# Four reduction pieces of each feed-forward output kept to the end and done token tile by token tile, in a four-block float32 transformer kernel

## The chip, the cores and the metric

One core of a Trainium2 chip runs the whole program in one launch. The metric is the device time of one execution in microseconds (us), the median over several executions. TensorE is written PE in the profile (its weight loads PEld), VectorE is DVE, ScalarE is ACT, GpSimd is POOL and SyncE is SP.

## What is computed

The input x has 256 tokens of 1024 features. It goes through two blocks of a first kind and then two of a second kind, everything in float32. Cut to what matters here:

```python
# first kind, twice
x = layer_norm(ALPHA * x + mix, ln1_g[i], ln1_b[i])              # mix: attention and spatial gating
gate, up = jnp.split(x @ w_ffn_in[i], 2, axis=-1)                # D_FF = 2816
ffn = (jax.nn.silu(gate) * up) @ w_ffn_out[i]
ple = (p[i] @ w_ple[i]) * jax.nn.sigmoid(x @ w_ple_gate[i])
x = layer_norm(ALPHA * x + ffn + ple, ln2_g[i], ln2_b[i])
# second kind, twice
mod = silu(c) @ ada_w[layer] + ada_b[layer]                      # sh1, sc1, g1, sh2, sc2, g2
h = rms_norm(x, norm_mix[layer]) * (1 + sc1) + sh1
x = x + g1 * mixer(h)
h = rms_norm(x, norm_mlp[layer]) * (1 + sc2) + sh2
a = jax.nn.relu(h @ mlp_w1[layer])                               # 4096 wide
x = x + g2 * ((a * a) @ mlp_w2[layer])
```

## The kernel before, in words

**Tokens and matmuls.** The 256 tokens are two token tiles t = 0 and 1 of 128. A product of float32 precision is made of three matmuls: an operand is divided into a high part (the rounded value) and a low part (the rest), and high x high, high x low and low x high are added in PSUM (lines 1375 to 1377). The activations transposed for this lie in XTH/XTL (the stage's input, 8 pieces of 128 features) and HTH/HTL (the feed-forward's inner values, 8 pieces).

**Weights.** All weights are streamed from HBM once, in the order of `plan()` (line 46). A chunk of the plan is cut into items of at most 2048 elements per partition (1 MB). There are 9 buffers of that size (NBUF, line 20); RAW and WB are two views of the same memory. SP loads an item into one buffer (`load`, line 1262). `split` then uses a second buffer: ACT writes the high part into it (line 1501, recorded as line 1497, WB<-RAW) and DVE replaces the raw value by the low part (line 1699). An item in use therefore holds two buffers, until its last matmul, and an item that is only loaded holds one.

**The planner.** The order of every instruction is written out once by the Python code: `do(part, ...)` appends to one list, and each engine executes its own part of that list in this order. `advance()` (line 312) splits items ahead of their use until `cur["ahead"]` reaches `cur["pairs"]`, which is 3. `loads()` (line 304) puts loads into the list ahead of that; its condition is quoted here, because the change touches what it gives:

```python
while cur["load"] < len(seq) and most and cur["load"] - cur["item"] < NBUF - 2 * cur["pairs"] and bufs:
```

With `pairs` 3 this lets 9 - 6 = 3 loads lie ahead of the item that is split next. A load waits only for what frees its own buffer, but SP issues loads in list order. `used()` (line 338) gives an item's two buffers back with the event of its last matmul.

**The ada items.** The weights of the `mod` product are not for PE. They are items of 1 MB as well, put one by one behind other items (lines 275 to 287), and DVE multiplies them into an accumulator with four instructions (`ada`, lines 1745 to 1760; source lines 1755 and 1758). An ada item has no split; when the planner comes to it, it appends the ada step to the list and its buffer is free again when DVE has done it. There are 8 ada chunks of two items in each first-kind feed-forward and 8 in the first second-kind MLP; the second MLP has none.

**A feed-forward of the first kind** (lines 836 to 896). For c = 0 to 10 the input product of chunk c (two items of w_ffn_in, 24 matmuls each over both tiles) is made; between its two items the inner values of chunk c-1 are transposed (`ffn_turn`, source line 1400 on PE, ACT makes HTH, DVE makes HTL at line 1780). After it `partial()` (line 455) adds chunk c-1 times w_ffn_out (one item, 24 matmuls) into four PSUM banks. Its inner values come out of PSUM by ACT (Silu, GB<-ps) and DVE (line 1994). In all pieces but the last two, `partial` does an item for both tiles. The last two, d = 9 and 10, are done at the end tile by tile: both items for tile 0, `last(0)`, both items for tile 1, `last(1)`. `last` adds the sum to x (line 2002), and takes the layer norm: statistics (1961, 1964), reciprocal root on POOL (1297, 1299), and two passes (1971, 1974). The transposition of tile 0's result for the next stage stands between tile 1's statistics and its passes (`between`, line 880). In the second layer (i = 1) it is not a plain transposition: `norm_tile` (648) squares x on ACT, takes the root on POOL and scales x into MIX on DVE (1979), and `go` (662) transposes MIX and applies scale and shift, half on ACT and half on DVE (1800), before XTH and XTL (1805) are made.

**An MLP of the second kind** (lines 1198 to 1246) is built alike with 8 chunks: two items of mlp_w1 and two of mlp_w2 per chunk, each transposition two halves (1.0 us of PE), Relu and Square on ACT. Only the last piece, d = 7, is done tile by tile; `last` multiplies by the gate and adds (2058, 2062).

**The joint.** The next stage starts in `linear2` (line 411): its first item for tile 0, then `mid()`, which holds the transposition of tile 1, then more of tile 0, then tile 1. `pad` is a number of 128x512 matmuls on constants whose result is not used (`busy`, source line 1360); they stand ahead of a wait.

## Time and profile before

| what | value |
|---|---|
| median of 3 executions | 1452.9 us |
| lowest and highest of these | 1451.3 and 1455.47 us |
| the profiled execution, its own time | 1450.07 us |
| its span, first to last instruction | 1448.3 us |
| mean granted TensorE clock | 0.981 |
| busy, share of the span: PE, PEld, DVE, ACT, POOL | 93, 77, 65, 45 and 8% |
| read from HBM | 267.75 MB, 186 GB/s over the span |

The profile covers one execution. Its times are us from the span's start unless ns is said. "idle before <-releaser" names what an engine waited for. The granted clock is a share of full speed: 1.00 is 2.4 GHz and 0.50 is 1.2 GHz. Matmuls overlap, so the step from one start to the next counts, not the recorded duration.

### The profile page before, as it was taken

What the parts mean: (1) busy time and instruction counts of PE and PEld (TensorE: products, weight loads), DVE (VectorE), ACT (ScalarE), POOL (GpSimd) and SP (SyncE); (2) the same over time, 40 slices, a digit from 0 to 9 for tenths busy, and PEclk for the clock granted to TensorE, in tenths of its full rate; (3) what the DMA queues carried; (4) which work ended last, traced back from release to release, by engine and by line L of the source; (5) the groups of instructions that cost most, each with busy time, mean ns of one, the idle gap of its engine ahead of it and who ended that gap; (6) DMA issues with size and microseconds to landing.
All of it is one profiled execution on the core that took longest, in us unless ns stands there. A gap on an engine that the chain in (4) does not pass through costs nothing.

```text
span 1448.3 us, 16560 instructions
## 1 busy us (share of the span) xinstructions
PE 1352.1 (93%) x6683; PEld 1111.1 (77%) x6715; DVE 943.2 (65%) x1249; ACT 656.9 (45%) x886; POOL 113.7 (8%) x156
## 2 busy tenths in 40 slices
PE   6999999999989999999789898999998978899998
PEld 6767888887967788887589776888876766688886
DVE  4856777766675777774657856766765775554444
ACT  4544533333553543334366444544435544454542
POOL 1010000000020000000223300000003330000000
PEclk9999999999999999999999999999999988999999
DMA  8505677772713567774153204776753430355550
GB/s 345 209 1 203 231 292 290 293 285 98 269 59 116 207 260 291 291 298 181 41 192 135 102 1 145 269 284 248 281 225 141 151 115 1 116 203 178 188 186 29
DMA packets 40236, 269.87 MB, mean 186 GB/s; under 512 B 4544, under 2 KB 4688, under 8 KB 11872
## 3 DMA queue, kind: packets, MB, share of 16 engines
q1 hardware_dynamic: 37712, 259.31, 48.1%
q0 software_dynamic: 2304, 8.46, 1.6%
q8 instruction: 53, 0.87, 0.2%
q10 hardware_dynamic: 144, 1.05, 0.2%
q14 instruction: 23, 0.19, 0.0%
HBM read 267.75 MB, written 1.05 MB: 186 GB/s over the span
## 4 chain that ended last, share of the span: by engine, by line
PE 78%; DVE 11%; ACT 5%; issue 2%; POOL 2%; DMA 1%; DVEq 0%; ACTq 0%; POOLq 0%
PE ps L1375 23%; PE ps L1377 23%; PE ps L1376 23%; PE ps L1400 4%; DVE WB L1699 2%; ACT E L1497 1%; PE ps L1484 1%; PE ps L1388 1%; POOL st L1299 1%; ACT WB L1497 1%; PE ps L1460 1%; DVE st L1893 1%; PE ps L1360 1%; ACT XTH L1497 1%; DVE st L1961 1%
## 5 line engine op out<-in xcount | busy, mean ns | idle before, releaser
L1699 DVE TENSOR_TENSOR WB<-RAW,WB 128x2048 fp32r<-128x2048 f32 (+5 forms) x210 | 453.3, 2161 | 271.7 <-ACT WB L1497 271.5
L1375 PE MATMUL ps<-WB,XTH 128*128 128x512 f32 (+3 forms) x1176 | 457.3, 389 | 33.3 <-DVE XTL L1704 14.0
L1497 ACT ACTIVATE WB<-RAW 128x2048 fp32r<-128x2048 f32 (+5 forms) x210 | 379.8, 1809 | 237.5 <-PE ps L1377 223.1
L1377 PE MATMUL ps<-WB,XTL 128*128 128x512 f32 (+3 forms) x1176 | 447.9, 381 | 0.0
L1376 PE MATMUL ps<-WB,XTH 128*128 128x512 f32 (+3 forms) x1176 | 447.2, 380 | 0.0
L1375 PEld LDWEIGHTS ps<-WB,XTH 128*128 128x128 f32 x1176 | 222.7, 189 | 75.7 <-DVE XTL L1704 14.0
L1377 PEld LDWEIGHTS ps<-WB,XTL 128*128 128x128 f32 x1176 | 222.5, 189 | 38.7
L1376 PEld LDWEIGHTS ps<-WB,XTH 128*128 128x128 f32 x1176 | 223.0, 190 | 34.8
L1375 PE MATMUL ps<-WB,HTH 128*128 128x512 f32 (+1 forms) x452 | 179.3, 397 | 3.2 <-DVE HTL L1780 3.2
L1376 PE MATMUL ps<-WB,HTH 128*128 128x512 f32 (+1 forms) x452 | 178.5, 395 | 0.0
L1377 PE MATMUL ps<-WB,HTL 128*128 128x512 f32 (+1 forms) x452 | 178.5, 395 | 0.0
L1758 DVE SCALAR_TENSOR_TENSOR ACC<-RAW,colv,ACC 128x512 f32<-128x512 f32 x168 | 126.2, 751 | 5.1
L1497 ACT ACTIVATE HTH<-ps 128x512 fp32r<-128x512 f32 (+1 forms) x58 | 32.1, 585 | 163.3 <-PE ps L1400 163.1
L1297 POOL TENSOR_SCALAR st<-st 128x1 f32<-128x1 f32 (+3 forms) x42 | 25.6, 610 | 1016.1 <-DVE st L1964 540.4
L1375 PEld LDWEIGHTS ps<-WB,HTH 128*128 128x128 f32 x452 | 85.9, 190 | 22.7 <-DVE HTL L1780 3.7
L1377 PEld LDWEIGHTS ps<-WB,HTL 128*128 128x128 f32 x452 | 85.8, 190 | 19.6
L1376 PEld LDWEIGHTS ps<-WB,HTH 128*128 128x128 f32 x452 | 86.0, 190 | 19.1
L1497 ACT ACTIVATE GB<-ps 128x512 f32<-128x512 f32 (+1 forms) x94 | 46.5, 500 | 91.6 <-PE ps L1377 91.5
L1497 ACT ACTIVATE E<-ps,st 128x128 f32<-128x128 f32 (+1 forms) x104 | 42.5, 421 | 80.1 <-DVE st L1903 80.1
L1360 PE MATMUL ps<-cstb 128*128 128x512 bf16 x227 | 64.4, 401 | 1.9 <-issue 0.2
L1780 DVE TENSOR_TENSOR HTL<-ps,HTH 128x512 fp32r<-128x512 f32 x54 | 35.8, 688 | 39.9 <-ACT HTH L1497 39.9
L1299 POOL TENSOR_TENSOR st<-st,cst 128x1 f32<-128x1 f32 (+3 forms) x42 | 48.1, 1145 | 3.5
(173 smaller groups left out, 1055.2 us busy)
## 6 DMA issues: line engine op xcount, KB each, us to landing
RAW<-W SPq DMA_DIRECT2D x220, 1024.0 KB, 4.9
RAW<-W SPq DMA_DIRECT2D x7, 960.0 KB, 4.7
RAW<-W SPq DMA_DIRECT2D x6, 910.0 KB, 6.5
RAW<-W SPq DMA_DIRECT2D x9, 576.0 KB, 3.5
VEC<-vecd POOLq DMA_DIRECT2D x10, 512.0 KB, 6.0
RAW<-W SPq DMA_DIRECT2D x8, 512.0 KB, 3.3
RAW<-W SPq DMA_DIRECT2D x6, 546.0 KB, 7.0
GB<-xTd ACTq DMA_DIRECT2D x1, 1024.0 KB, 8.4
```

The costliest lines, as they stand in the source:

```text
L1297: eng.tensor_scalar(x, x, scale, eps, ALU.mult, ALU.add).then_inc(*own.up())
L1299: eng.tensor_tensor(x, x, MH.to_broadcast([128, x.shape[1]]), ALU.pow).then_inc(*up("rsqrt", key))
L1360: eng.matmul(banks[b][:, :], identb, cstb[:, 0:512], start=True, stop=True)
L1375: eng.matmul(ps, xh, hi[:, j, c0:c0 + cw], start=first and j == 0, stop=False)
L1376: eng.matmul(ps, xh, lo[:, j, c0:c0 + cw], start=False, stop=False)
L1377: op = eng.matmul(ps, xl, hi[:, j, c0:c0 + cw], start=False, stop=last and j == n - 1)
L1388: op = eng.matmul(banks[b][:, q:q + 1], ACC[:, a, q * 128:q * 128 + 128], ones[:, 0:1], start=True, stop=True)
L1400: op = eng.transpose(banks[b][0:rows, j * 128:j * 128 + 128], src, ident)
L1497: return eng.activation(dst, src, f, **k)
L1699: eng.tensor_tensor(WB[:, it["raw"], 0:w], RAW[:, it["raw"], 0:w], WB[:, it["high"], 0:w].bitcast(F32), ALU.subtract).then_inc(*up("wl", n))
L1758: op = eng.scalar_tensor_tensor(out=ACC[:, a, :], in0=view[:, j, :], scalar=cond[:, kt:kt + 1], in1=ACC[:, a, :], op0=ALU.mult, op1=ALU.add)
L1780: eng.tensor_tensor(HTL[:, r2:r2 + 2, :], banks[b][:, :].rearrange("p (n q) -> p n q", n=2), HTH[:, r2:r2 + 2, :].bitcast(F32), ALU.subtra ...
```

## The change

The plan keeps the w_ffn_out pieces 7 to 10 to the end (before, 9 and 10 alone were done tile by tile, and every piece had its place in the plan behind the input product of the next chunk), and the mlp_w2 pieces 6 and 7 (before: 7). The last `partial` has then four items per tile in all three kinds of stage. From c = 8 (first kind) and c = 6 (second kind) `cur["pairs"]` is 4, until the last `partial` is over. `partial` takes a table `before` of steps that are put in front of item n of tile t: the last transposition in front of (0, 1) or (0, 2), splits of the next stage in front of (1, 1), the second half of the normalisation in front of (1, 2), and tile 0's transposition for the next stage in front of (1, 3). The pads of 14, 10, 11 and 6 matmuls at the joints become 3, 3, 3 and 2; the pad of 11 ahead of each MLP stays.

```diff
@@ plan()
-            if c:
-                out.append(("w_ffn_out", i, (c * 256 - 256, c * 256), [(0, 1024)]))
+            for d in [c - 1] if 0 < c <= 7 else range(7, 11) if c == 11 else []:
+                out.append(("w_ffn_out", i, (d * 256, d * 256 + 256), [(0, 1024)]))
...
-            if c:
-                out.append(("mlp_w2_2", i, (c * 512 - 512, c * 512), [(0, 1024)]))
+            for d in [c - 1] if 0 < c <= 6 else range(6, 8) if c == 8 else []:
+                out.append(("mlp_w2_2", i, (d * 512, d * 512 + 512), [(0, 1024)]))
@@ partial()
-        def partial(name, parts, ps, first, last, evac=None):
+        def partial(name, parts, ps, first, last, evac=None, before={}):
...
                     for n in range(len(its)):
+                        if (t, n) in before:
+                            before[t, n]()
                         one(n, t)
@@ norm_tile()
-        def norm_tile(t, after):
+        def norm_start(t, after):
             g = uid()
             ss = col(1)
             do("norm_sq", g, t, ss, after)
             do("rsqrt", ("nt", g), ss, 1.0 / D, 1e-6, ("norm_sq", g))
+            return g, t, ss
+
+        def norm_end(g, t, ss):
             do("norm_apply", g, t, ss)
             hn[t] = ("hn", g)
+
+        def norm_tile(t, after):
+            norm_end(*norm_start(t, after))
@@ start of the second layer
-                run(linear2("w_in", "x", xt_w, puts[0:2], mid_in, pad=(6, 0)))
+                run(linear2("w_in", "x", xt_w, puts[0:2], mid_in, pad=(2, 0)))
@@ feed-forward of the first kind
+            for c in range(11):
+                if c == 8:
+                    cur["pairs"] = 4
...
+                gen = linear("w_ffn_in", "x", xt_w, put)
+                next(gen)
                 if c:
-                    d = c - 1
...
-                if c < 11:
-                    run(gen)
+                    part_ = ffn_turn(c - 1)
+                run(gen)
                 if c:
...
-                    if d < 9:
-                        ht_free[d % 2] = [partial("w_ffn_out", [part_], acc4, d == 0, False)]
-                    elif d == 9:
-                        part9 = part_
+                    if c - 1 < 7:
+                        ht_free[(c - 1) % 2] = [partial("w_ffn_out", [part_], acc4, c == 1, False)]
+                    else:
+                        kept.append(part_)
...
+            kept.append((4, []))
...
+            def turn_last():
+                kept[-1][1].extend(ffn_turn(10)[1])
+                gb_free[:] = f_free[0] + [("ffn", (i, 10, 0)), ("ffn", (i, 10, 1))]
+                if i:
+                    do("lambdas", col(2), list(scr["free"]))
+                    scr["free"] = [("lam_dot", 0)]
+                    then["mod"] = norm_mod(0, 0, list(gb_free))
+
+            def tile0():
+                if i:
+                    then["mod"][1](0, pad=3)
+                else:
+                    xt_w[0][:] = to_XT(X, 8, x_n[0], 0)
 
             def last(t, done):
...
-                def between():
-                    if t and i == 0:
-                        xt_w[0][:] = to_XT(X, 8, x_n[0], 0)
-                    elif t:
-                        norm_tile(0, x_n[0])
-                        go(0, pad=14)
-
-                x_n[t] = ln_tile((i, 2, t), t, [("add_out", (i, t, c)) for c in range(2)], between)
-                if t:
-                    advance(1)
-                if t and i == 1:
-                    norm_tile(1, x_n[1])
-
-            t_pe = [partial("w_ffn_out", [part9, part_], acc4, False, True, last)]
+                x_n[t] = ln_tile((i, 2, t), t, [("add_out", (i, t, c)) for c in range(2)])
+                if i:
+                    then["norm"] = norm_start(t, x_n[t])
+                    if t:
+                        norm_end(*then["norm"])
...
+            t_pe = [partial("w_ffn_out", kept, acc4, False, True, last,
+                            {(0, 1): turn_last, (1, 1): lambda: advance(1),
+                             (1, 2): (lambda: norm_end(*then["norm"])) if i else lambda: advance(1), (1, 3): tile0})]
+            cur["pairs"] = 3
@@ starts of the two second-kind layers
-                            pad=(10, 0)))
+                            pad=(3, 0)))
...
-                                                                  for c in range(2)], mid, pad=(11, 0)), part((2, 3))),
+                                                                  for c in range(2)], mid, pad=(3, 0)), part((2, 3))),
@@ MLP of the second kind
+            gen = linear2("mlp_w1_2", "x", xt_w, [put_f(0), put_f(1)], mid, pad=(11, 0))
+            next(gen)
+            for c in range(1, 8):
+                if c == 6:
+                    cur["pairs"] = 4
...
+                part_ = mlp_turn(c - 1)
+                run(gen)
...
+                if c - 1 < 6:
+                    ht_free[(c - 1) % 2] = [partial("mlp_w2_2", [part_], acc4, c == 1, False)]
...
+            kept = [part_, (4, [])]
+
+            def turn_last():
+                kept[1][1].extend(mlp_turn(7)[1])
+                if i == 0:
+                    then["mod"] = norm_mod(1, 0, f_free[1] + [("sq", (0, 7, 0)), ("sq", (0, 7, 1))])
 
             def last(t, done):
-                if t and i == 0:
-                    go(0)
                 for c in range(2):
                     gated_put(i, c, 1, xg)(t, acc4[t][c][0], done[c])
-                if t:
-                    advance(1)
-                if i == 0:
-                    norm_tile(t, xg[t])
+                if i:
+                    do("store", t, xg[t])
                 else:
-                    do("store", t, xg[t])
-
-            t_pe = [partial("mlp_w2_2", [part_], acc4, False, True, last)]
+                    then["norm"] = norm_start(t, xg[t])
+                    if t:
+                        norm_end(*then["norm"])
+
+            before = {(0, 2): turn_last}
+            if i == 0:
+                before.update({(1, 1): lambda: advance(1), (1, 2): lambda: norm_end(*then["norm"]),
+                               (1, 3): lambda: then["mod"][1](0, pad=3)})
+            t_pe = [partial("mlp_w2_2", kept, acc4, False, True, last, before)]
+            cur["pairs"] = 3
```

`mlp_turn` is the old transposition of a chunk as a function, and `ffn_turn` in the first kind likewise.

## Rows read from the trace of the kernel before

**Rows 1.** The page: busy time of each engine, share of the span, instructions.
```profile
PE 1352.1 (93%) x6683; PEld 1111.1 (77%) x6715; DVE 943.2 (65%) x1249; ACT 656.9 (45%) x886; POOL 113.7 (8%) x156
```

**Rows 2.** Timeline of PE, joint after the first feed-forward (start, us, idle before).
```profile
339.63 0.63 PE L1400 MATMUL ps<-cst,GB 128*128 128x128 f32 x4 [1.02 <-DVE GB L1994]
...
351.06 0.40 PE L1377 MATMUL ps<-WB,HTL 128*128 128x512 f32 x1
...
358.45 1.04 PE L1400 MATMUL ps<-cst,X 128*128 128x128 f32 x8
```

**Rows 3.** Timeline of PE, joint after the second feed-forward.
```profile
694.07 0.40 PE L1377 MATMUL ps<-WB,HTL 128*128 128x512 f32 x1
...
701.25 1.09 PE L1400 MATMUL ps<-cst,MIX 128*128 128x128 f32 x8 [3.75 <-DVE MIX L1979]
...
707.61 0.41 PE L1375 MATMUL ps<-WB,XTH 128*128 128x384 f32 x1 [1.42 <-DVE XTL L1805]
...
713.01 1.09 PE L1400 MATMUL ps<-cst,MIX 128*128 128x128 f32 x8 [2.08 <-DVE MIX L1979]
```

**Rows 4.** Timeline of PE, first MLP: its last transposition's product and the joint.
```profile
1078.65 0.47 PE L1375 MATMUL ps<-WB,HTH 128*128 128x512 f32 x1 [1.62 <-DVE HTL L1780]
...
1089.89 1.04 PE L1400 MATMUL ps<-cst,MIX 128*128 128x128 f32 x8
...
1102.51 1.97 PE L1400 MATMUL ps<-cst,MIX 128*128 128x128 f32 x8 [2.92 <-DVE MIX L1979]
```

**Rows 5.** Chain that ended last: small products at chunk ends, first feed-forward and first MLP.
```profile
291.50 0.79 PE ps L1388 x8
...
309.37 0.79 PE ps L1388 x8
...
1027.54 0.79 PE ps L1388 x8
...
1051.41 0.79 PE ps L1388 x8
```

**Rows 6.** Timeline of DVE at the start of chunk 8, first feed-forward.
```profile
293.55 2.29 DVE L1699 TENSOR_TENSOR WB<-RAW,WB 128x2048 fp32r<-128x2048 f32 x1 [1.06 <-ACT WB L1497]
295.76 0.48 DVE L1755 TENSOR_SCALAR ACC<-RAW,colv 128x512 f32<-128x512 f32 x1
296.28 2.33 DVE L1758 SCALAR_TENSOR_TENSOR ACC<-RAW,colv,ACC 128x512 f32<-128x512 f32 x3
298.96 0.69 DVE L1780 TENSOR_TENSOR HTL<-ps,HTH 128x512 fp32r<-128x512 f32 x1 [0.36 <-ACT HTH L1497]
...
302.98 3.11 DVE L1758 SCALAR_TENSOR_TENSOR ACC<-RAW,colv,ACC 128x512 f32<-128x512 f32 x4
```

**Rows 7.** SP's waits, 290 to 310 us; landing of two loads then; of the last load.
```profile
SPq L1266 <- DVE ACC L1758: 13.4, 2, 6.7
...
DMA to landing us min/median/max: 4.8/5.9/6.9
...
DMA to landing us min/median/max: 4.8/4.8/4.8
```

**Rows 8.** Groups by line and shape: count, then busy us, mean ns of one.
```profile
L1497 ACT ACTIVATE WB<-RAW 128x2048 fp32r<-128x2048 f32 x172 | 329.0, 1913 | 192.9 <-PE ps L1377 188.2 <-DMA RAW<-W 4.6
...
L1497 ACT ACTIVATE GB<-ps 128x256 f32<-128x256 f32 x44 | 17.0, 385 | 57.6 <-PE ps L1377 57.6
L1994 DVE TENSOR_TENSOR GB<-GB,ps 128x256 f32<-128x256 f32 x44 | 16.9, 415 | 5.8 <-ACT GB L1497 5.8
...
L1497 ACT ACTIVATE GB<-GB 128x512 f32<-128x512 f32 x32 | 20.2, 632 | 1.0
L1497 ACT ACTIVATE MIX<-X 128x1024 f32<-128x1024 f32 x8 | 8.5, 1059 | 28.6 <-DVE X L2062 17.8 <-DVE X L1974 10.8
```

**Rows 9.** Granted clock by stretch of 1 us, the column before the last two.
```profile
1102.00:1103.00 1.00, 0.49 (x3) 0.49 (x4) 1.00 (x2) 0.00 (x0) 1.00 (x2) 0.50 0.00 0
...
1105.00:1106.00 1.00, 1.00 (x5) 0.77 (x5) 0.13 (x1) 0.81 (x2) 1.00 (x4) 0.83 0.00 0
```

More of the change, by code:

```diff
@@ L835, in program, with ffn_turn, put @@
             acc4 = None
-            for c in range(12):
-                if c < 11:
-                    def put(t, b, done, c=c):
-                        do("ffn", (i, c, t), t, c, b, done, f_free[c % 2])
-                        give(b, ("ffn", (i, c, t)))
-                    gen = linear("w_ffn_in", "x", xt_w, put)
-                    next(gen)
-                if c:
-                    d = c - 1
-                    r2 = 2 * (d % 4)
-                    b, fr = take()
-                    g = uid()
-                    do("ffn_turn", g, [GB[:, t, (d % 2) * 256 + kt * 128:(d % 2) * 256 + kt * 128 + 128]
-                                       for kt in range(2) for t in range(2)], r2, b,
-                       [("ffn", (i, d, t)) for t in range(2)] + fr, ht_free[d % 2])
-                    give(b, ("tl", g))
-                    f_free[d % 2] = [("tp", g)]
-                if c < 11:
-                    run(gen)
+            kept = []
+            def ffn_turn(d):
+                r2 = 2 * (d % 4)
+                b, fr = take()
+                g = uid()
+                do("ffn_turn", g, [GB[:, t, (d % 2) * 256 + kt * 128:(d % 2) * 256 + kt * 128 + 128]
+                                   for kt in range(2) for t in range(2)], r2, b,
+                   [("ffn", (i, d, t)) for t in range(2)] + fr, ht_free[d % 2])
+                give(b, ("tl", g))
+                f_free[d % 2] = [("tp", g)]
+                return r2, [("tl", g)]
+            for c in range(11):
+                if c == 8:
+                    cur["pairs"] = 4
+                def put(t, b, done, c=c):
+                    do("ffn", (i, c, t), t, c, b, done, f_free[c % 2])
+                    give(b, ("ffn", (i, c, t)))
+                gen = linear("w_ffn_in", "x", xt_w, put)
+                next(gen)
+                if c:
+                    part_ = ffn_turn(c - 1)
+                run(gen)
                 if c:
@@ L1196, in put_f, with mlp_turn @@
                 return put
-            for c in range(9):
-                if c == 0:
-                    gen = linear2("mlp_w1_2", "x", xt_w, [put_f(0), put_f(1)], mid, pad=(11, 0))
-                    next(gen)
-                    continue
-                if 2 <= c < 8:
+            def mlp_turn(d):
+                los = []
+                for hf in range(2):
+                    b, fr = take()
+                    g = uid()
+                    r2 = 4 * (d % 2) + 2 * hf
+                    do("ffn_turn", g, [GB[:, t, (d % 2) * 512 + (hf * 2 + kt) * 128:(d % 2) * 512 + (hf * 2 + kt) * 128 + 128]
+                                       for kt in range(2) for t in range(2)], r2, b,
+                       [("sq", (i, d, t)) for t in range(2)] + fr, ht_free[d % 2])
+                    give(b, ("tl", g))
+                    los.append(("tl", g))
+                f_free[d % 2] = [("tp", g)]
+                return 4 * (d % 2), los
@@ L1204, in program @@
+            gen = linear2("mlp_w1_2", "x", xt_w, [put_f(0), put_f(1)], mid, pad=(11, 0))
[3 more added lines that the diff above has]
+                    cur["pairs"] = 4
+                if c > 1:
                     gen = linear("mlp_w1_2", "x", xt_w, put_f(c))
                     next(gen)
[L1206 to L1218 removed]
@@ new lines, in program @@
+                run(gen)
+                if acc4 is None:
+                    acc4 = [[take(), take()], [take(), take()]]
+                if c - 1 < 6:
+                    ht_free[(c - 1) % 2] = [partial("mlp_w2_2", [part_], acc4, c == 1, False)]
+            xg = [[], []]
+            then = {}
+            kept = [part_, (4, [])]
[3 more added lines that the diff above has]
+                    then["mod"] = norm_mod(1, 0, f_free[1] + [("sq", (0, 7, 0)), ("sq", (0, 7, 1))])
@@ L1244, in program @@
+            before = {(0, 2): turn_last}
[4 more added lines that the diff above has]
+            cur["pairs"] = 3
+            if i == 0:
+                mod, go = then["mod"]
             x_w = xg
```

40 lines of the change are left out of this document (7 added, 33 removed).

## The prediction

> **What bounds the kernel now.** I read the page first: PE is busy for 93% of 1448.3 us [rows 1], so a gain can only come from the gaps of PE. The timeline of PE shows where they are. Inside the weight-streaming stages there are none: a chunk takes 17.9 us from one small product to the next, which is three items of 5.6 us and the transposition and small product, 1.1 us, and in the first MLP 23.9 us, four items of 5.5 us and 1.8 us [rows 5]. The gaps that the change is about lie at the joints. After the first feed-forward, 1.0 us ahead of the last transposition, and 7.15 us from the last product's end (351.3) to tile 1's transposition (358.45) [rows 2]. After the second, 18.7 us from 694.3 to 713.01, only part of it work [rows 3]. After the first MLP, 12.6 us from 1089.89 to 1102.51 [rows 4]. The end of the program has no joint behind it.
>
> Then I read what feeds PE. SP waits for DVE's ada work, two waits of 6.7 us in 20 us [rows 7], and DVE shows a split (2.3), an ada step (2.9), HTL, a split and the next ada step (3.1) [rows 6]. With three loads ahead nobody notices that wait. That is the row to look at, because the change takes the loads ahead from three to one.
>
> **Part 1, `pairs` 4.** In the quoted condition 9 - 2x4 is 1. A load enters the list only when everything loaded has been split or, for an ada item, done. Two pairs of buffers freed by one item now both become high parts. I follow the list from chunk 8 of the first feed-forward, where M = 291.5 us is the end of piece 6 [rows 5]. In8a and in8b are split, in9a, ada A and in9b are loaded. The list becomes: split in9a, ada A, split in9b, load ada B, ada B, load in10a. Load ada B uses ada A's buffer, load in10a uses ada B's. DVE ends ada A at 298.65, as before [rows 6]. Then in series: ada B lands 4.8 later, the time of a lone 1 MB load [rows 7], at 303.5; DVE has it done 3.1 later at 306.6 [rows 6]; in10a lands 4.8 later at 311.4; its ACT half ends at 313.3 [rows 8]. In ACT's list the split of in10a stands ahead of the Silu of chunk 8, and on DVE its low half stands ahead of line 1994. So: ACT 313.3, DVE low half 315.6, two products 316.5 [rows 6, 8]. PE wants them for the transposition of chunk 8, behind in9a, at 292.3 + 3x5.6 + 0.35 = 309.4. It stands idle for 7.1 us. Behind it, in10a and in10b are split in time and no later load has an ada item in front: no further stall in this stage.
>
> After such a gap the clock is low. Once PE had stood for nearly 3 us, the clock was 0.50 (1.2 GHz) from 1102 and was back by about 1105.3 [rows 4, 9]: 3.3 us at half speed, 1.6 us lost. The sum takes 1.6 for each long gap that ends a chain; its bounds are 0 (no drop) and 3.3 (twice as long). Both feed-forwards have ada items at chunk 8, so 2 x (7.1 + 1.6) = **17.4 us**.
>
> The sum by a lone load's 4.8 us is for the last load of the program. The Trainium skill (DMA: Bandwidth & Descriptors, Anatomy of one DMA) fits another issuing path with about 2.0 us plus bytes at 436 GB/s, which would be 4.4 us; by it the seven serial loads counted here and below would cost 2.8 us less in all.
>
> **Part 2, the first MLP.** M = 1027.5 is the end of the second item of piece 4 [rows 5]. The same list: ada A done M + 7.1, ada B landed 11.9, done 15.1, in7a landed 20.0. HTL of chunk 5 stands behind ada B: 16.4, PE wants it at 0.8 + 5.5 + 1.0 + 5.5 = 12.8, with the real gaps 12.6: 3.8 us. Then ada items stand between pieces 6a and 6b and behind it. The load of the first waits for piece 5a (M + 22.3) and DVE is through at 33.9; 6b lands 38.8, ACT 40.7, DVE 43.0, second ada 46.1, HTL of chunk 6 47.4. PE wants it at 40.4: 7.0 us. Piece 7a is loaded into that ada's buffer and lands at 51.0, ACT 52.9; four Relu and Square of 0.63 [rows 8] 55.4; PE wants the last transposition at 53.0: 2.4 us. HTL 7 comes behind the split of 7b, at 61.0, against 56.5: 4.5 us, of which 1.6 is there now [rows 4], because this transposition stands in front of (0, 2) and is needed at once. Sum 3.8 + 7.0 + 2.4 + 2.9 = 16.1, and one drop of the clock, 1.6; earlier drops fall into the next wait: **17.7 us**. These are list orders times row durations; the links are bounded by 0 (all hidden) and by landing times of 6.9 instead of 4.8 us, which the second of two loads close together has [rows 7], some 2 us for each of seven loads.
>
> **Part 3, the joints.** Moving products does not change their number; tile 1 has now four items, 11.2 us, beside tile 0's chain. But the joint ends with tile 1's chain, which is as long as before.
> *First joint.* The last transposition no longer waits: gain 1.2 with its issue. Tile 1's chain loses the 1.2 us of XTL halves from its middle and starts some 0.3 late: 6.2 instead of 7.15 [rows 2]. Tile 0's transposition, 1.05 us, now stands in the products. Net gain 1.2 - 1.05 + 0.95 = 1.1, say 1.2 with the shorter pad.
> *Second.* The split put in front of (1, 1) stands on ACT behind tile 0's square (1.06) [rows 8] and on DVE ahead of tile 0's scaling: norm 6.25 (as long as tile 1's 6.2 above), square 7.45, ACT split 9.25, DVE 11.45, scaling 12.2 us after tile 0's last product. PE reaches tile 0's transposition at 8.4 + pad 0.7 = 9.1: a new stall of 3.1. From the new end of the products tile 1's transposition follows 11.9 us later instead of 18.7 [rows 3]; that end is 1.05 + 0.7 + 3.1 later, and 1.2 are saved at the last transposition: 18.7 - 11.9 - 4.85 + 1.2 = 3.1. Three splits, not two, are then ahead of tile 1's scale and shift: -1.1. Gain 2.0.
> *Third.* Tile 1's transposition follows 8.3 instead of 12.6 us [rows 4] after the products; the end is 1.75 later: 2.5. Behind it PE waits 1.2 for a split and 2.5 for XTL, where it now loses 0.6: together a loss of 0.6.
> *Fourth, the program's end:* no ada items in that MLP; a load is issued at an item's end, lands 4.8 us later and is wanted after 5.5. The wait of 1.6 stays. 0.
> Joints: **-2.6 us**, bounded by 0 and by -12 (if no split were in the way). Pads: fewer constants, 0 on the path, since each stands in a wait.
>
> **Sum.** 17.4 + 17.7 - 2.6 = 32.5. On the profiled execution's 1450.07 that is 1482.6; it lies 2.8 below the median, and the forecast is 1452.9 + 32.5, about **1485 us**.
>
> **Rivals.**
> *A: the first MLP hides its chain,* since its chunk is 6 us longer than the feed-forward's for the same two ada items [rows 5]. Against: HTL stands behind ada B in DVE's list whatever the chunk's length. 1452.9 + 17.4 - 2.6 = 1468. 0.09.
> *B: faster.* The place is DVE's ada B at chunk 8: if its load were already under way, PE sees no gap, and only the joints change; with tile 0's normalisation covered by 11.2 us and splits out of its way they give up to 12: 1441; with my own joints 1450. It decides at 7 us: the chain from ada A's end to the GB product is 17.8 us long and must shrink to 10.7. For it: today SP's waits cost nothing. Against: the condition allows one load. 0.11 in all, 0.07 of it beyond 0.3%.
> *C: the clock falls more.* The pads of 14 and 11 at the joints are gone and each joint keeps a wait of 3 to 6 us; already with pads it fell once [rows 9]. Five more half-speed stretches at 1.6 and some loads at 6.9: 1485 + 8 + 6 = 1499. 0.12. By the Trainium skill (TensorE: Matmul & The Clock Gate, What's actually happening) the throttled clock is the default and activity releases it; that rule speaks for this rival.
>
> **How the numbers follow.** Forecast 0.68, A 0.09, B 0.11, C 0.12. A measurement tells 0.3%, 4.4 us, from no change. Faster 0.07, same 0.04, slower 0.89. The forecast's own bounds are 1485 - 1.6x3 - 9 (joints) = 1471 and 1485 + 15 = 1500; with A in, 1466 to 1500. B and the far ends of C are left out.
>
> **What would show it.** In the profile after: a wait of PE at line 1400 for DVE GB of 6 to 8 us at chunk 8 of both feed-forwards, ACT waiting for DMA just ahead of it, DVE's ada step waiting for DMA; HTL waits of 4, 7 and 4.5 us in the first MLP; no 1.0 us wait at the feed-forwards' last transposition, the 1.6 one left in both MLPs; granted clock below 0.981. The prediction is wrong if PE has no wait at chunk 8 of the feed-forwards, or if ACT never waits there for DMA.

## The result, and the profile after

The changed kernel takes **1484.7 us** (median of 4 runs, 1483.4 to 1488.8), the kernel before 1452.1 (4 runs, 1450.9 to 1455.5): a ratio of 1.0225, with a 95% interval of 1.0207 to 1.0242. It is 32.6 us slower. The chips differ by up to 2 us, so each experiment has its own runs of the kernel before. The profiled execution of the changed kernel took 1485.46 us and has a span of 1483.7.

The page of the changed kernel, first the line that answers to [rows 1], then the share of the chain that ended last, then three groups of section 5:

```profile
PE 1365.6 (92%) x6688; PEld 1122.1 (76%) x6688; DVE 942.3 (64%) x1249; ACT 655.4 (44%) x886; POOL 118.2 (8%) x156
...
PE 72%; DVE 14%; ACT 6%; DMA 4%; issue 3%; POOL 2%; SPq 0%; ACTq 0%; DVEq 0%; POOLq 0%
...
L1407 PE MATMUL ps<-WB,XTH 128*128 128x512 f32 (+3 forms) x1176 | 462.2, 393 | 31.4 <-DVE XTL L1736 14.2
...
L1407 PE MATMUL ps<-WB,HTH 128*128 128x512 f32 (+1 forms) x452 | 182.7, 404 | 13.5 <-DVE HTL L1812 13.5
...
L1790 DVE SCALAR_TENSOR_TENSOR ACC<-RAW,colv,ACC 128x512 f32<-128x512 f32 x168 | 126.2, 751 | 13.9 <-DMA RAW<-W 8.8
```

DVE and ACT do the same work in the same time. PE has the same products, but 27 fillers fewer at the joints: 41 before, 14 now, since the third joint has also got 3 ahead of tile 0's transposition, where it had none. (The counts of the page, 6688 and 6683, do not show this, as some records of products are missing from a trace.) A filler takes 0.21 us from one start to the next, by the first of these two groups of PE's timeline at the third joint. It is of the kernel before, the second of the changed one:

```profile
1090.98 2.32 PE L1360 MATMUL ps<-cstb 128*128 128x512 bf16 x10
...
1124.87 0.81 PE L1392 MATMUL ps<-cstb 128*128 128x512 bf16 x3
```

So PE had 5.8 us less to do, and it is busy for 13.5 us longer all the same (1365.6 against 1352.1 in [rows 1]): its products run slower. PE's busy time inside the stretches with a granted clock of 0.50, halved, is what they lost: 22.4 us before and 41.3 after, 18.9 more. The span grew by 35.4 us, of which 21.9 are time in which PE is idle. DMA has 4% of the chain, which had 1% of it before.

The waits of ACT for loads, over the whole execution (total us, times, longest), and then those of PE for the two tiles that the forecast named. Lines are shifted by the change: 1407 to 1409 are the products, 1432 the transpositions, 1812 HTL, 2026 the GB product, 1731 and 1529 the two halves of a split, 1787 and 1790 the ada step.

```profile
ACT WB L1529 <- DMA RAW<-W: 83.6, 18, 12.7
```

```profile
PE ps L1407 <- DVE HTL L1812: 15.0, 6, 4.3
...
PE ps L1432 <- DVE GB L2026: 12.3, 2, 6.2
```

Before, ACT waited for loads 7 times, 14.2 us in all, the longest 6.6; PE 3.2 us for HTL and 2.0 for GB. The chain of waits can be read at chunk 8 of the first feed-forward. The timeline of DVE, which answers to [rows 6]:

```profile
296.37 2.29 DVE L1731 TENSOR_TENSOR WB<-RAW,WB 128x2048 fp32r<-128x2048 f32 x1 [1.05 <-ACT WB L1529]
298.58 0.48 DVE L1787 TENSOR_SCALAR ACC<-RAW,colv 128x512 f32<-128x512 f32 x1
299.09 2.33 DVE L1790 SCALAR_TENSOR_TENSOR ACC<-RAW,colv,ACC 128x512 f32<-128x512 f32 x3
...
306.33 3.11 DVE L1790 SCALAR_TENSOR_TENSOR ACC<-RAW,colv,ACC 128x512 f32<-128x512 f32 x4 [2.71 <-DMA RAW<-W]
309.37 0.68 DVE L1812 TENSOR_TENSOR HTL<-ps,HTH 128x512 fp32r<-128x512 f32 x1
316.22 2.29 DVE L1731 TENSOR_TENSOR WB<-RAW,WB 128x2048 fp32r<-128x2048 f32 x1 [6.17 <-ACT WB L1529]
318.43 0.74 DVE L2026 TENSOR_TENSOR GB<-GB,ps 128x256 f32<-128x256 f32 x2
```

The timeline of ACT there, and that of PE:

```profile
314.28 1.91 ACT L1529 ACTIVATE WB<-RAW 128x2048 fp32r<-128x2048 f32 x1 [12.53 <-DMA RAW<-W]
316.10 0.64 ACT L1529 ACTIVATE GB<-ps 128x256 f32<-128x256 f32 x2
```

```profile
310.10 0.50 PE L1407 MATMUL ps<-WB,XTH 128*128 128x512 f32 x1 [0.77 <-DVE HTL L1812]
...
319.32 1.08 PE L1432 MATMUL ps<-cst,GB 128*128 128x128 f32 x4 [6.17 <-DVE GB L2026]
```

Ada A ends at 301.4. Ada B starts when its load lands, at 306.33, 4.9 us later, and ends at 309.4; the load of in10a, which uses its buffer, lands at 314.28, again 4.8 later. Only then do ACT, DVE and at last PE go on. From the small product (PE has its last product before it until 294.33) to the end of the GB products there are 24.9 us.

To see where the time went, take one instruction of PE that both kernels have and compare its start. This table is worked out from the timelines of PE; "added" is the step of the difference from the row above.

| instruction of PE | before | after | difference | added |
|---|---|---|---|---|
| first small product of the first feed-forward | 184.12 | 186.94 | 2.8 | 2.8 |
| transposition of H after the first joint | 388.01 | 399.13 | 11.1 | 8.3 |
| first small product of the second feed-forward | 527.15 | 538.75 | 11.6 | 0.5 |
| transposition of MIX after the second joint | 731.90 | 749.94 | 18.0 | 6.4 |
| first small product of the first MLP | 914.24 | 930.67 | 16.4 | -1.6 |
| transposition of modc after the third joint | 1123.87 | 1156.52 | 32.6 | 16.2 |
| end | 1448.3 | 1483.7 | 35.4 | 2.8 |

The three changed places that bring time are worth 8.3 + 6.4 + 16.2 = 30.9 us. The other 4.5 arise in the rows between, where both kernels do the same but for the second MLP, in the last one. What the slow clock took from PE's busy time grew by 14.4 us in the three rows and by 4.5 in the others, so the granted clock, which fell at other moments (below), accounts for them. The medians, which average over that, differ by 32.6.

The three waits of the first MLP, in the timeline of PE (the second and the third answer to [rows 4]), with the transposition between them:

```profile
1061.03 0.77 PE L1407 MATMUL ps<-WB,HTH 128*128 128x512 f32 x1 [4.34 <-DVE HTL L1812]
...
1091.27 0.76 PE L1407 MATMUL ps<-WB,HTH 128*128 128x512 f32 x1 [3.71 <-DVE HTL L1812]
...
1099.55 1.03 PE L1432 MATMUL ps<-cst,GB 128*128 128x128 f32 x8
...
1104.40 0.77 PE L1407 MATMUL ps<-WB,HTH 128*128 128x512 f32 x1 [3.81 <-DVE HTL L1812]
```

The joints, which answer to [rows 2] (tile 1's transposition) and [rows 3] (tile 0's and tile 1's), again in PE's timeline:

```profile
362.32 0.40 PE L1409 MATMUL ps<-WB,HTL 128*128 128x512 f32 x1
...
368.77 1.06 PE L1432 MATMUL ps<-cst,X 128*128 128x128 f32 x8 [3.07 <-DVE X L2006]
...
714.10 1.43 PE L1432 MATMUL ps<-cst,MIX 128*128 128x128 f32 x8 [2.64 <-DVE MIX L2011]
...
719.18 0.39 PE L1409 MATMUL ps<-WB,HTL 128*128 128x512 f32 x1
...
729.71 1.97 PE L1432 MATMUL ps<-cst,MIX 128*128 128x128 f32 x8 [5.95 <-DVE MIX L2011]
```

From the last product's end to tile 1's transposition there are 6.05 us at the first joint (7.0 before) and 10.1 at the second (18.5 before). The joints did get shorter; and tile 0's transposition at the second waits for 2.64 us.

The granted clock (the column before the last two), in stretches of 1 us, at chunk 8 and after the wait of the first joint:

```profile
321.00:322.00 1.00, 1.00 (x4) 0.74 (x3) 0.98 (x2) 1.00 (x2) 0.00 (x0) 0.50 0.01 0
...
324.00:325.00 1.00, 1.00 (x6) 0.82 (x5) 1.00 (x1) 0.38 (x1) 0.00 (x0) 1.00 0.00 0
369.00:370.00 1.00, 1.00 (x10) 1.00 (x9) 1.00 (x1) 0.57 (x2) 0.00 (x0) 0.99 0.00 0
370.00:371.00 1.00, 1.00 (x5) 1.00 (x5) 1.00 (x2) 0.52 (x2) 0.00 (x0) 0.50 0.00 0
...
373.00:374.00 1.00, 1.00 (x6) 1.00 (x6) 0.00 (x0) 0.00 (x0) 0.57 (x1) 0.80 0.00 0
```

At 0.50 (1.2 GHz) PE does 4 or 5 instructions in 1 us, at 1.00 (2.4 GHz) 6 to 10. Summed over all stretches of 1 us from 10 us on, what is missing to 1.00 comes to 27.9 us before and 51.4 after; part of it lies in waits, where it costs nothing, and the 41.3 and 22.4 us above are the part in which PE was at work.

### The profile page after: what moved, and what is told of

Read it like the earlier page. It is cut to its first block, busy times and chain, and to the rows that moved or that the text cites. A ratio compares the mean times of both kernels' runs of the same rounds, so it can differ in the third digit from the quotient of the medians.

```text
span 1483.7 us, 16531 instructions
## 1 busy us (share of the span) xinstructions
PE 1365.6 (92%) x6688; PEld 1122.1 (76%) x6688; DVE 942.3 (64%) x1249; ACT 655.4 (44%) x886; POOL 118.2 (8%) x156
## 4 chain that ended last, share of the span: by engine, by line
PE 72%; DVE 14%; ACT 6%; DMA 4%; issue 3%; POOL 2%; SPq 0%; ACTq 0%; DVEq 0%; POOLq 0%
PE ps L1407 21%; PE ps L1409 21%; PE ps L1408 21%; PE ps L1432 4%; DMA RAW<-W 4%; DVE WB L1731 3%; ACT WB L1529 2%; DVE ACC L1790 2%; ACT E L1529 1%; PE ps L1516 1%; PE ps L1420 1%; PE ps L1492 1%; PE ps L1392 1%; POOL st L1331 1%; DVE st L1925 1%
## 5 line engine op out<-in xcount | busy, mean ns | idle before, releaser
L1407 PE MATMUL ps<-WB,XTH 128*128 128x512 f32 (+3 forms) x1176 | 462.2, 393 | 31.4 <-DVE XTL L1736 14.2
L1407 PEld LDWEIGHTS ps<-WB,XTH 128*128 128x128 f32 x1176 | 225.8, 192 | 74.5 <-DVE XTL L1736 14.6
L1408 PEld LDWEIGHTS ps<-WB,XTH 128*128 128x128 f32 x1176 | 225.8, 192 | 35.3
L1407 PE MATMUL ps<-WB,HTH 128*128 128x512 f32 (+1 forms) x452 | 182.7, 404 | 13.5 <-DVE HTL L1812 13.5
L1408 PE MATMUL ps<-WB,HTH 128*128 128x512 f32 (+1 forms) x452 | 180.8, 400 | 0.0
L1407 PEld LDWEIGHTS ps<-WB,HTH 128*128 128x128 f32 x452 | 87.7, 194 | 34.1 <-DVE HTL L1812 14.7
L1408 PEld LDWEIGHTS ps<-WB,HTH 128*128 128x128 f32 x452 | 87.6, 194 | 19.6
```

Of the source, the lines that this page charges most:

```text
L1407: eng.matmul(ps, xh, hi[:, j, c0:c0 + cw], start=first and j == 0, stop=False)
L1408: eng.matmul(ps, xh, lo[:, j, c0:c0 + cw], start=False, stop=False)
```

## The experiments

All ratios are to the kernel before on the same chip.

### Which term is which: the switch to four pairs, later

**e1.** Both switches are moved, 8 to 10 in the feed-forwards and 6 to 7 in the MLPs.

```
-                if c == 8:
+                if c == 10:
                     cur["pairs"] = 4
...
-                if c == 6:
+                if c == 7:
                     cur["pairs"] = 4
```

> The changed kernel with one edit: the four pairs start at chunk 10 instead of 8 in both feed-forwards, and at chunk 7 instead of 6 in both MLPs. Everything else of the change stays. Theory S (the stalls come from loads that go one by one past the ada items): in the feed-forwards the GB wait of 6.2 us, the HTL wait of 0.8 and the slow products behind them (1.4) vanish, 2 x 8.3 = 16.6 us; in the first MLP the wait for the HTL of chunk 5 (4.3) and its slow products (2.5) vanish, and of the two later ones (3.7 and 3.8, with 4 us of slow products) at least half goes, since the loads of the first ada item and of piece 6b are under way before the switch: 7 + 5 = 12. 1484.7 - 16.6 - 12 = 1456, within 1450 to 1462. Rival K (the kept pieces and the splits packed ahead of the joints cost the time, whenever the switch comes): no less than 1475.

**e2.** Only the first of the two edits.

> The same edit in the two feed-forwards alone (chunk 10 instead of 8); the MLPs keep the switch at chunk 6. It parts the two terms of the prediction. Theory S: 1484.7 - 16.6 = 1468, and the three HTL waits of the first MLP stay at 4.3, 3.7 and 3.8 us. If the MLP's share were small (rival A of the prediction), e1 and this one would agree within 3 us.

Measured: e1 1458.2 us (10 runs, ratio 1.0030, 1.0018 to 1.0043), e2 1465.9 us (4 runs, ratio 1.0084, 1.0058 to 1.0111). So the late switch in the feed-forwards alone gives back 18.8 us of the 32.6 (16.6 expected), and that in the MLP another 7.7 (12 expected). Taken against the kernel before on the same chip, e2 gives back 19.6. The sum for e1 was 1456, and 1458.2 is within its range. In e1's list of PE's waits no wait for DVE's GB is left, and of HTL this:

```profile
PE ps L1407 <- DVE HTL L1812: 9.4, 3, 4.2
```

The wait for the HTL of chunk 5 is gone, as expected. Those of chunks 6 and 7 are still there, in PE's timeline of e1:

```profile
1063.73 0.61 PE L1407 MATMUL ps<-WB,HTH 128*128 128x512 f32 x1 [3.59 <-DVE HTL L1812]
...
1071.65 1.07 PE L1432 MATMUL ps<-cst,GB 128*128 128x128 f32 x8 [0.55 <-ACT GB L1529]
...
1076.93 0.76 PE L1407 MATMUL ps<-WB,HTH 128*128 128x512 f32 x1 [4.22 <-DVE HTL L1812]
```

I had expected half of them to go. The last ada items stand between the kept pieces 6a, 6b and 7a, so the chain of single loads only starts one chunk later; e6 below takes them out of that place. Rival K, that the kept pieces themselves cost the time, wanted 1475 or more, and falls. Rival A of the prediction, that the MLP hides its chain, falls too: e1 and e2 differ by 7.7 us, and e2's waits of PE for HTL still come to 14.5 us, where the kernel before has 3.2.

### Four pairs without the kept pieces

**e3.** The kernel before, with the switch and its way back, at the places where the changed kernel has them.

```
             for c in range(12):
+                if c == 8:
+                    cur["pairs"] = 4
...
             t_pe = [partial("w_ffn_out", [part9, part_], acc4, False, True, last)]
+            cur["pairs"] = 3
...
             for c in range(9):
+                if c == 6:
+                    cur["pairs"] = 4
...
             t_pe = [partial("mlp_w2_2", [part_], acc4, False, True, last)]
+            cur["pairs"] = 3
```

> The kernel before with nothing but four pairs of buffers from chunk 8 of each feed-forward and chunk 6 of each MLP until their last partial is done; no piece is kept back. Theory S says where four pairs alone bite: in the MLP the list of items is the same in both kernels, so the three waits come here too, 12 to 16 us; in the feed-forward piece 7 still stands among the products of chunk 8 and gives the chain from the first ada step to the GB product (24.9 us after the small product) 5.7 us more cover, 22.8 instead of 17.1, so that 0 to 3 us are left for each: 1452 + 14 + 3 = 1469, within 1464 to 1475. Rival P (four pairs cost the same wherever they stand): 1482 or more. Rival K (the kept pieces cost it): 1452 to 1456.

Measured: 1475.3 us (4 runs, ratio 1.0142, 1.0111 to 1.0173), 22.4 us slower than before; expected were 17, and the range ended at 1475, so it is just outside. Compared by the same method as in the table, the MLP costs 13.8 us (12 to 16 expected) and each feed-forward 5.5 (0 to 3 expected). The miss is in the feed-forward. The timeline of DVE in e3 and the wait in that of PE:

```profile
300.17 2.28 DVE L1705 TENSOR_TENSOR WB<-RAW,WB 128x2048 fp32r<-128x2048 f32 x1
305.32 3.11 DVE L1764 SCALAR_TENSOR_TENSOR ACC<-RAW,colv,ACC 128x512 f32<-128x512 f32 x4 [2.86 <-DMA RAW<-W]
308.35 0.68 DVE L1786 TENSOR_TENSOR HTL<-ps,HTH 128x512 fp32r<-128x512 f32 x1
```

```profile
309.08 0.50 PE L1381 MATMUL ps<-WB,HTH 128*128 128x512 f32 x1 [3.64 <-DVE HTL L1786]
```

I had looked for the end of the chain, the GB product, and found it covered by piece 7. It is. But HTL of chunk 7 stands behind ada B in DVE's list, and piece 7 wants it at 305.45: a wait of 3.64 us, and its 24 products then take 7.4 us instead of 5.75. Without the kept pieces the single load costs 22 us; the change as a whole costs 33.

### The ada item or the single load

**e5.** The changed kernel with its switches where they are; only the ada chunks of the feed-forwards are moved one chunk forward in the plan.

```
-            if 1 <= c <= 8:
-                ada(*ADA[i * 8 + c - 1])
+            if c <= 7:
+                ada(*ADA[i * 8 + c])
```

> The changed kernel with the switch to four pairs left at chunk 8 and chunk 6; only the ada items of each feed-forward stand one chunk earlier (with chunks 0 to 7 instead of 1 to 8), so that none is left in the list once a single load goes ahead. Theory S (it is the ada item in the chain of single loads, not the single load by itself): the waits of 6.2 and 0.8 us at chunk 8 vanish in both feed-forwards, with their clock: as the run with the late switch in the feed-forwards, 1466, within 1463 to 1470. Rival L (one load ahead is too few for PE by itself, since a 1 MB load takes 4.8 us, ACT and DVE 4.1 and a piece of products 5.7): the waits move to chunks 9 and 10 and the time stays above 1475.

Measured: 1464.6 us (4 runs, ratio 1.0076, 1.0050 to 1.0102), 1466 expected. No wait for GB is among PE's, and its waits for HTL are the MLPs' alone (13.8 us). It is as good as e2, by an edit that does not touch the number of loads ahead. This settles the mechanism in the feed-forwards: one load ahead is enough for PE as long as every item in the list is split; the ada item, which has to be done before its buffer is free, turns it into a chain load, ada, load, split. Rival L (a single load is too little by itself) falls.

### The fillers

**e4.** The changed kernel with the fillers that stand in `linear2` at the three joints at their length of before. These are 19 of the 27 that the change took away. The 14 ahead of tile 0's transposition at the second joint stay at 3.

```
-                run(linear2("w_in", "x", xt_w, puts[0:2], mid_in, pad=(2, 0)))
+                run(linear2("w_in", "x", xt_w, puts[0:2], mid_in, pad=(6, 0)))
...
-                            pad=(3, 0)))
+                            pad=(10, 0)))
...
-                                                                  for c in range(2)], mid, pad=(3, 0)), part((2, 3))),
+                                                                  for c in range(2)], mid, pad=(11, 0)), part((2, 3))),
```

> The changed kernel with the lengths of the filler products at the three joints put back to those of before (6, 10 and 11 instead of 2, 3 and 3); the switch stays at chunk 8 and 6. Theory S: fillers lie in waits, no change beyond the clock: 1484.7 - 0 to 3. Rival C (the shorter fillers let the clock fall at the joints): the half-speed stretches at 370, 714, 728 and 1134 us go and the time falls by 5 us or more, to 1480 or less.

Measured: 1487.3 us (4 runs, ratio 1.0228, 1.0203 to 1.0253), not faster than the changed kernel (1.0225). In one place the clock did what rival C says: in e4 it stays up behind the wait of the first joint,

```profile
370.00:371.00 1.00, 0.78 (x7) 0.81 (x8) 1.00 (x2) 0.12 (x1) 0.00 (x0) 1.00 0.00 0
...
373.00:374.00 1.00, 1.00 (x8) 1.00 (x7) 1.00 (x3) 0.29 (x1) 0.13 (x1) 1.00 0.00 0
```

That the fillers held it there is not shown. In the profiled executions of e1, e2, e6 and e7 the clock stays at 1.00 behind the same wait (3.08 to 3.12 us) with the short fillers of the changed kernel; in those of e5 and e8, with the same fillers and the same wait (3.08), it falls, and in that of e10, with no filler and a wait of 3.54, it falls for 6.8 us. And ahead of that joint, at chunk 8, where nothing was edited, e4's clock falls for longer (5.1 us missing to 1.00 instead of 3.4). The total does not move: as a remedy, longer fillers in `linear2` do nothing.

### Removing what is left

**e6.** e1, and the 24 ada chunks spread 9, 9 and 6, where they were 8, 8 and 8.

```
-            if 1 <= c <= 8:
-                ada(*ADA[i * 8 + c - 1])
+            if c <= 8:
+                ada(*ADA[i * 9 + c])
...
-            if i == 0 and c < 8:
-                ada(*ADA[16 + c])
+            if i == 0 and c < 6:
+                ada(*ADA[18 + c])
```

> The run with the late switch in all stages (1458.2), and the 24 ada chunks spread 9, 9 and 6 over the chunks 0 to 8 of the feed-forwards and 0 to 5 of the first MLP, where they were 8, 8 and 8: none stands among the last pieces of the MLP. Theory S: the waits of the first MLP for the HTL of chunk 6 (3.6 us), for the Squares of chunk 7 (0.55) and for the HTL of chunk 7 (4.2, of which 1.6 was there before the change) fall to 1.6, with some 3 us of half-speed products: 1458.2 - 6.8 - 3 = 1448.5, within 1446 to 1451. Rival D (the single load, or the 11th chunk's DVE work with ada items in chunk 0, costs as much elsewhere): 1455 or more.

Measured: **1446.1 us** (6 runs, ratio 0.9956, 0.9942 to 0.9970), 12.1 us less than e1, at the lower end of the range of 1446 to 1451. So the mechanism holds in the first MLP too: without ada items among the single loads its waits are gone, and rival D falls. Of PE's waits for HTL the two of 1.6 us are left that the kernel before has:

```profile
PE ps L1407 <- DVE HTL L1812: 3.2, 2, 1.6
```

**e9.** The kernel before with this plan, nothing else.

> The kernel before with the plan of ada chunks of the last three runs (9, 9, 6) and nothing else: three pairs, no piece kept back. It tells whether the gain of 7 to 9 us of those runs comes from the kept pieces and joints or from the plan. Theory S: with three loads ahead no ada item was on PE's path before, so the plan alone changes nothing: 1453 within 1450 to 1455. Rival A2 (the plan is the gain): 1447 or less.

Measured: 1452.8 us (11 runs, 1447.2 to 1458.4; ratio 1.0007, 0.9991 to 1.0023). The plan alone does nothing that these runs can tell. The 7 us that e6 gains on the kernel before are therefore the work of the change itself, the kept pieces with their reordered joints and the shorter fillers; no run parts these two.

**e7.** e6, with the first split moved behind tile 0's scaling, at the second joint.

```
-                            {(0, 1): turn_last, (1, 1): lambda: advance(1),
-                             (1, 2): (lambda: norm_end(*then["norm"])) if i else lambda: advance(1), (1, 3): tile0})]
+                            {(0, 1): turn_last, (1, 1): (lambda: None) if i else lambda: advance(1),
+                             (1, 2): lambda: (norm_end(*then["norm"]) if i else None, advance(1)), (1, 3): tile0})]
```

> The run before this one with the first split ahead of the joint moved behind tile 0's scaling, in the second joint alone (both at the second of the four products of tile 1). Theory S: DVE and ACT no longer do a split between tile 0's square and its scaling, so PE's wait of 2.6 us for tile 0's MIX falls below 1 and the half-speed stretch behind it (1.4 us) goes: 3 to 4 us less than the run before, about 1445. Rival J (the split then delays tile 1's scaling by as much): no change within 1 us.

Measured: 1446.8 us (4 runs, ratio 0.9953, 0.9936 to 0.9970): no gain in the total over e6. At the place itself the edit did what it should. DVE in e6, around the scaling (line 2011), and in e7:

```profile
692.25 2.16 DVE L1731 TENSOR_TENSOR WB<-RAW,WB 128x1920 fp32r<-128x1920 f32 x1 [2.91 <-ACT WB L1529]
694.32 0.75 DVE L2011 TENSOR_SCALAR MIX<-X,st 128x1024 f32<-128x1024 f32 x1
```

```profile
692.94 0.75 DVE L2011 TENSOR_SCALAR MIX<-X,st 128x1024 f32<-128x1024 f32 x1 [2.13 <-POOL st L1331]
693.73 2.16 DVE L1731 TENSOR_TENSOR WB<-RAW,WB 128x1920 fp32r<-128x1920 f32 x1
```

PE's wait of 2.69 us for tile 0's MIX is gone, and from the feed-forward's last transposition to tile 1's there are 33.5 us instead of 36.3. The total does not show it: in the profiled execution of e7 35.9 us are missing to a clock of 1.00, in that of e6 25.6, and the difference lies behind the joint, where the two programs are the same. Rival J said that the scaling of tile 1 would be late by as much, and it is not. So the mechanism was right, and the forecast of 1445 was missed. By these two profiles the clock took back what the joint gave. The mean clocks of the single executions do not settle it: the two of e7 at 0.980 and 0.981 took 1446.4 us each, and the four of e6 at 0.981 and 0.982 took 1445.0 to 1446.1, no more; but the two of e7 at 0.975 and 0.976 took 1447.2 and 1447.7, and the two of e6 at 0.977 took 1449.2 and 1449.5. Where the gain of the joint goes stays open.

**e8.** e7, with the last transposition of the MLPs one product earlier.

```
-            before = {(0, 2): turn_last}
+            before = {(0, 1): turn_last}
```

> The run before this one with the last transposition of both MLPs one product earlier (at the second piece of tile 0, as in the feed-forwards, not at the third). Theory S: PE waits about 0.5 us for the Squares of the last chunk, and its HTL is ready before the third piece: the wait of 1.6 us in each MLP becomes 0.5: 2.2 us less than the run before, up to 5 with the clock. Rival Q (the Squares come later than that): no gain, within 1 us.

Measured: 1444.4 us (4 runs, ratio 0.9938, 0.9923 to 0.9953), 2.4 less than e7 (2.2 expected). PE in e8:

```profile
1061.99 1.04 PE L1432 MATMUL ps<-cst,GB 128*128 128x128 f32 x8
...
1066.09 0.47 PE L1407 MATMUL ps<-WB,HTH 128*128 128x512 f32 x1 [0.27 <-DVE HTL L1812]
```

The transposition does not wait, and HTL costs 0.27 us instead of 1.62. As that product stands there in both MLPs, it is worth 1.35 each.

**e10.** e8 with the fillers at the three joints at length zero (leaving out `pad` in the two calls that transpose tile 0 and in the three `linear2` calls of e4).

> The best version so far (1444.4) with the filler products of the three joints at zero length (5 fillers of 0.8 us around tile 0's transpositions and 3 ahead of the next stage). Theory S: where PE waits anyway a filler is free and without one the clock may fall; tile 0's transpositions do not wait, so 0.65 us comes back at each of two places and at XTL's waits nothing: 1443 to 1445 if the clock stays. Rival C (fillers hold the clock): 3 us or more slower, 1447 and up, with more half-speed stretches at the joints.

Measured: 1443.8 us (5 runs, 1440.8 to 1446.2; ratio 0.9937, 0.9917 to 0.9958), the same as e8, and rival C's 1447 is not reached. Fillers of 0 and of 3 do not differ, and those of 11 (e4) bring nothing.

## Why the prediction was right, point by point

**The forecast, 1485, is 0.3 us from the median,** and the sum of 32.5 from the difference of 32.6. That is closer than its terms deserve, and in part luck. The chain of loads and the places were right. But at the three changed places the sum had three drops of the clock, 4.8 us, and the rows show 14.4 us lost to it; it had 27.7 us of waits, net of the joints, and PE's idle time grew by 22.7 there while 5.8 us of fillers went, 16.9 net. Two misses of some 10 us cancel.

Two rows were read a little high: the last products of [rows 2] and [rows 3] end at 351.46 and 694.47, so the gaps to tile 1's transposition were 7.0 and 18.5 us, not 7.15 and 18.7. That is about 0.3 us in the sum.

**Part 1, 17.4 us forecast.** Right in mechanism and size. The link-by-link chain to the end of the GB products was 25.0 us, measured 24.9. Per feed-forward the forecast was 7.1 of wait and 1.6 of clock; measured 6.94 of wait (6.17 for GB, and 0.77 earlier for the bank that the HTL of chunk 7 gives back) and 1.4 of slow products: the 24 products behind the wait take 6.7 us instead of 5.7 and the transposition 0.4 more. Twice 8.3 is 16.6. By experiment, e2 gives 18.8 and e5 20.1 (1484.7 less their medians), or 19.6 and 21.1 against the kernel before on the chip of each, which includes clock outside the feed-forwards. The step "no later load has an ada item in front" holds: no further wait in that stage.

The 4.8 us for a lone load were right (4.9 and 4.8 here). The estimate of 4.4 us by the fit in the Trainium skill (DMA: Bandwidth & Descriptors, Anatomy of one DMA), which is for another issuing path, is low by 0.4 to 0.5 us for each of them; the prediction went by the trace's row.

**Part 2, 17.7 us forecast.** Right in place and sum, with the size shared out otherwise. HTL of chunk 5: 3.8 forecast, 4.34 measured. HTL of chunk 6: ready 47.4 us after the end of piece 4 by the chain, measured 1091.2 - 1044.0 = 47.2; but PE comes 3.2 us later than I had it, because its 48 products after the first wait ran 2.5 us slower and that wait was 0.5 longer. So the wait is 3.7 and not 7.0. The wait for the Squares of chunk 7 (2.4) is not there, for the same reason: PE was held up by 3.7 + 2.7 us first. HTL of chunk 7: 4.5 forecast, 3.8 measured, 1.6 of it old. The waits come to 10.2 us more than before, not 16.1, and the slow products to 2.5 + 2.7 + 1.3 = 6.5, not 1.6: 16.7. The step that failed is "earlier drops fall into the next wait", in its size: a drop does shorten the wait behind it, but I had put its price at nothing and the whole wait into the sum. As the chain of loads kept its length (47.2), what the products lost the waits gave back, and the sum came out.

**Part 3, -2.6 us forecast.** *First joint:* 6.2 us from the last product to tile 1's transposition forecast, 6.05 measured, and no wait at the last transposition. But then the clock falls while PE is already at work (the rows at 370 us). From tile 1's transposition to that of H both kernels do the same, in 29.6 us before and 30.4 after, so it takes 0.8 back. The joint as a whole comes to 8.3 - 8.3 = 0, forecast -1.2. *Second:* a new wait of 3.1 at tile 0's transposition forecast, 2.64 measured; 11.9 from the products' end to tile 1's forecast, 10.1 measured, with a slow stretch on either side. Net 6.4 - 8.2 = -1.8, forecast -2.0. e7 shows that the reason given for the new wait, the split ahead of the scaling, is the right one. *Third:* tile 1's transposition starts 8.2 us after the products, 8.3 forecast, but the wait for XTL behind it is 0.9 and not 2.5; 16.2 - 16.7 = -0.5, forecast +0.6. *Fourth:* the wait of 1.6 stays; 0, as forecast. Sum -2.3, forecast -2.6; without the first joint's clock it would be -3.1. "Pads: 0 on the path" has no run for the 14 at the second joint; e4 and e10 bear it out for the others.

**What the sum did not have:** 4.5 us outside the three places, 2.8 of them ahead of the first changed instruction. They belong to this pair of executions: just ahead of the first feed-forward the ten profiles of the experiments stand between 0.1 us earlier and 2.8 later than that of the kernel before, which itself is 2 us below its median.

**The rivals.** A (the MLP hides its chain, 1468) fell by the MLP's own three waits, and by e2. B (faster; the chain must shrink to 10.7 us) fell, as the chain was 24.9; but its premise was right: with the chain taken away (e6) and the splits out of the way (e7, e8) the same joints give 1444, between its 1441 and 1450. C (the clock falls more, 1499) was right about the clock, with 14.4 us at the three places where the forecast had 4.8 and C 12.8, and wrong about the time, as the waits were shorter by about as much. Its cause, the missing fillers, is not borne out: longer ones do nothing (e4), and none at all cost nothing (e10).

**The signs named beforehand:** the GB wait of 6 to 8 us in both feed-forwards (6.17 and 6.11), ACT waiting for DMA ahead of it, DVE's ada step waiting for DMA, no wait at the feed-forwards' last transposition, a granted clock below 0.981 (0.965): all there. The HTL waits of 4, 7 and 4.5 were 4.3, 3.7 and 3.8.

## What to carry to other kernels

When a change lends buffers to one use, ask what the loads lose by it, and follow the list of loads item by item at the smaller number: an item that must be finished before its buffer is free (here an ada step, not a split) turns loads that ran side by side into a chain, 4.8 us each, and the engines' in-order lists carry its lateness to tiles that have nothing to do with it. Such a chain can be undone without giving up the change: borrow later, or move those items out of the stretch; here both together turn +2.2% into -0.4%, and -0.6% with a split and a transposition moved. And read an edit at its place as well as in the total, since other places can hide 3 us of gain or loss, as in e7.

## What the runs showed of the hardware

- In the profiled executions of kernels that differ by little, TensorE's granted clock goes to 0.50 at different places, most of them far from any edit. What is missing to 1.00 is 25.6 us in e6, 35.9 in e7 and 27.9 in the kernel before, 51.4 in the changed one. In these four profiles every fall but the one at the very end lasts 3.4, 6.8 or 10.2 us at 0.50, as that from 370.0 to 373.4 us in the changed kernel.
- The fall can come after the wait: at the first joint PE waits until 368.77, runs at 0.99 to 370 and only then for 3.4 us at 0.50. It does not fall there in e4, with 4 filler products more ahead of the wait, nor in e1, e2, e6 and e7, with as few as in the changed kernel; it does in e5 and e8, with the same number, and in e10, with none. The Trainium skill (TensorE: Matmul & The Clock Gate, What's actually happening) has activity as what releases the clock; here the clock falls after PE has gone back to work, and no run here shows what decides that.
- A slow stretch in front of a wait whose end is set by a chain of loads costs little in the total, as it shortens the wait: in the first MLP the waits came out 5.9 us shorter than the chain of rows said, and the slow products 4.9 us longer.
